# Down projections of a one-core transformer kernel: who makes the weight sums, and what tells TensorE that the token sums are there

## The reference

```
def swiglu(h, w1, w3, w2):
    return (jax.nn.silu(h @ w1) * (h @ w3)) @ w2

def conv_ffn(xn, w_up, conv_w, conv_b, w_down):
    h = causal_depthwise_conv(xn @ w_up, conv_w) + conv_b
    g, u = jnp.split(h, 2, axis=-1)
    return (jax.nn.gelu(g) * u) @ w_down
```

## Time and profile before

| | us |
|---|---|
| three executions | 2795.14, 2795.41, 2796.20 |
| the profiled execution, whole | 2793.67 |
| its span | 2791.9 |
| TensorE busy | 2723.3 (98%) |
| VectorE busy | 1519.2 (54%) |
| ScalarE busy | 471.2 (17%) |
| GpSimd busy | 109.4 (4%) |
| TensorE's share of the chain that ended last | 94% |

### The profile page before, as it was taken

How to read it: one execution, slowest core, us unless ns; L and a number is a source line. 1 busy time by engine, 2 the same in 40 slices (tenths; PEclk the granted TensorE clock), 3 DMA queues, 4 the chain that set the end, 5 groups by cost and what they waited for, 6 DMA issues and landing times.

```text
span 2791.9 us, 38954 instructions
## 1 busy us (share of the span) xinstructions
PE 2723.3 (98%) x16184; PEld 2459.8 (88%) x16184; DVE 1519.2 (54%) x3134; ACT 471.2 (17%) x827; POOL 109.4 (4%) x98
## 2 busy tenths in 40 slices
PE   7999999999999999999999999999999999999998
PEld 6899899888889999889878899988888998887888
DVE  4687765453457666466563466535335652323565
ACT  1011332321100100242132100003210011111000
POOL 0000000000000340000000131000000000000000
PEclk9999999999999999999999999999999999999999
DMA  9886621325886444441132444442324444342442
GB/s 368 316 320 253 236 91 61 114 100 178 296 303 259 161 167 167 165 149 48 61 121 106 165 168 167 156 163 104 136 106 152 159 157 151 129 146 96 154 159 95
DMA packets 74720, 460.78 MB, mean 165 GB/s; under 512 B 8340, under 2 KB 9248, under 8 KB 28208
## 3 DMA queue, kind: packets, MB, share of 16 engines
q1 hardware_dynamic: 73408, 451.44, 44.6%
q0 software_dynamic: 1136, 6.86, 0.7%
HBM read 457.17 MB, written 1.09 MB: 164 GB/s over the span
## 4 chain that ended last, share of the span: by engine, by line
PE 94%; DVE 3%; DVEq 1%; ACT 1%; DMA 1%; issue 0%; ACTq 0%
PE psum L514 20%; PE psum L560 16%; PE psum L706 14%; PE psum L646 9%; PE psum L873 8%; PE psum L947 4%; PE psum L758 4%; PE psum L595 2%; PE psum L582 2%; PE psum L661 2%; PE psum L893 2%; PE psum L823 1%; PE psum L770 1%; PE psum L536 1%; PE psum L846 1%; PE psum L836 1%
## 5 line engine op out<-in xcount | busy, mean ns | idle before, releaser
L514 PE MATMUL psum<-h,ring 128*128 128x256 f32 x1648 | 358.8, 379 | 3.1 <-DVE h L1978 1.7
L514 PEld LDWEIGHTS psum<-h,ring 128*128 128x128 f32 x1648 | 312.5, 190 | 47.8 <-DVE h L1978 2.5
L560 PE MATMUL psum<-aring,ring 128*128 128x256 f32 x1408 | 304.7, 379 | 1.7 <-issue 1.7
L560 PEld LDWEIGHTS psum<-aring,ring 128*128 128x128 f32 x1408 | 267.4, 190 | 38.7 <-issue 2.4
L706 PE MATMUL psum<-arena 128*128 128x128 f32 x2112 | 249.7, 275 | 1.1 <-DVE arena L1624 1.1
L706 PEld LDWEIGHTS psum<-arena 128*128 128x128 f32 x2112 | 242.6, 192 | 1.3 <-DVE arena L1624 1.3
L873 PE MATMUL psum<-h,ring 128*128 128x256 f32 x1024 | 231.1, 382 | 0.0
L873 PEld LDWEIGHTS psum<-h,ring 128*128 128x128 f32 x1024 | 193.2, 192 | 26.9 <-issue 1.9
L706 PE MATMUL psum<-arena,ring 128*128 128x128 f32 x1584 | 191.6, 275 | 0.0
L706 PEld LDWEIGHTS psum<-arena,ring 128*128 128x128 f32 x1584 | 184.4, 192 | 0.2
L514 PE MATMUL psum<-arena,ring 128*128 128x256 f32 x720 | 157.7, 380 | 6.0 <-DVE arena L2331 3.1
(11 more groups left out here) (417 smaller groups left out, 3567.2 us busy)
## 6 DMA issues: line engine op xcount, KB each, us to landing
ring<-wstream SPq DMA_DIRECT2D x351, 1024.0 KB, 4.8
aring<-astream SPq DMA_DIRECT2D x128, 512.0 KB, 5.3
arena<-astream SPq DMA_DIRECT2D x16, 512.0 KB, 18.0
arena<-wstream SPq DMA_DIRECT2D x3, 1024.0 KB, 20.5
arena<-decays POOLq DMA_DIRECT2D x2, 1024.0 KB, 7.7
sq<-decays POOLq DMA_DIRECT2D x2, 1024.0 KB, 5.2
kst<-const SPq DMA_DIRECT2D x1, 1280.5 KB, 7.9
x<-xT SPq DMA_DIRECT2D x1, 1024.0 KB, 4.9
```

Source lines behind the costliest of these rows:

```text
L514: mm = pe.matmul(out, lhsT=tile_at(at[0] % RING, t), rhs=rhs(k), start=k == 0, stop=k == kt - 1)
L560: mm = pe.matmul(psum[:, s % 4, n * T:(n + 1) * T], lhsT=tile_at(slot, n * KD + k), rhs=rhs(k), start=k == 0, stop=k == KD - 1)
```

## The change

All four weight sums of a down slab are made by GpSimd, in a new function `down_weight_sums`, which is put into GpSimd's queue at the place where each of the six rounds comes in the program. VectorE's `weight_sums` and its calls go. The semaphore `weights_summed` is split: `down_summed` (GpSimd, two signals a slab: third and fourth sum) and `hidden_ready` (VectorE, two signals a round: token sums up to hidden slab 15, and the last ones). TensorE waits for `down_summed` ahead of M6 and M3, for `hidden_ready` at slabs 0 and 2.

```
+            def down_weight_sums(rounds):
+
+                first = first_down[rounds]
+                for j in range(11):
+                    i = first + j
+                    w = ring[:, i % RING].rearrange("p (a t) -> p a t", a=4)
+                    new = down_sums[:, j % 2].rearrange("p a u t -> p a (u t)")
+                    pool.wait_ge(landed[i % RING], landing(i))
+                    if j >= 2:
+                        pool.wait_ge(slab_used, i - 1)
+                    nc.gpsimd.tensor_tensor(new[:, 0], w[:, 2], w[:, 3], ALU.add)
+                    nc.gpsimd.tensor_tensor(new[:, 1], w[:, 0], w[:, 2], ALU.subtract)
+                    pool.drain()
+                    nc.gpsimd.tensor_tensor(new[:, 2], new[:, 0], w[:, 0], ALU.subtract).then_inc(down_summed, 1)
+                    pool.drain()
+                    nc.gpsimd.tensor_tensor(new[:, 3], w[:, 1], new[:, 2], ALU.subtract).then_inc(down_summed, 1)
...
+            down_weight_sums(0)
             decay_rows(0)
+            down_weight_sums(1)
             for s in range(2, NF):
                 weight_sums(quick_up[0], s)
+            down_weight_sums(2)
             decay_rows(1)
             pool.wait_ge(arena_free, 1)
             pool.dma_start(memx, memT).then_inc(mem_in, 16)
             for s in range(2, NF):
                 weight_sums(quick_up[1], s)
+            down_weight_sums(3)
             for layer, n in ((0, FH), (1, LH)):
...
+                down_weight_sums(4 + layer)
...
                     if j == 0:
-                        pe.wait_ge(weights_summed, 34 * rounds + 1)
+                        pe.wait_ge(hidden_ready, 2 * rounds + 1)
...
                     if j == 2:
                         fresh()
-                        pe.wait_ge(weights_summed, 34 * rounds + 7)
+                        pe.wait_ge(hidden_ready, 2 * rounds + 2)
...
-                            need = dict(M6=2, M5=2, M7=2, M3=3).get(name, 0)
-                            if need and p == mine[0][0]:
-                                pe.wait_ge(weights_summed, 34 * rounds + 3 * j + need + (j >= 2))
+                            if name in ("M6", "M3") and p == mine[0][0]:
+                                pe.wait_ge(down_summed, 22 * rounds + 2 * j + (1 if name == "M6" else 2))
...
                 if s % 4 == 3:
                     D()
-                    token_sums(hidden, down_tokens, s // 2 - 1, 2)
-                if s in (18, 20):
-                    D()
-                    weight_sums(first, s // 2 - 9)
+                    last = token_sums(hidden, down_tokens, s // 2 - 1, 2)
+                    if s == 15:
+                        last.then_inc(hidden_ready, 1)
                 if s == NF - 1:
                     D()
-                    token_sums(hidden, down_tokens, s // 2, 1).then_inc(weights_summed, 1)
+                    token_sums(hidden, down_tokens, s // 2, 1).then_inc(hidden_ready, 1)
...
-                first = cnt.value("slab_used")
                 for j in range(11):
-                    if j + 2 < 11:
-                        weight_sums(first, j + 2)
```

More of the change, by code:

```diff
@@ L318, in build @@
         roots_read = sem("roots_read")
-        weights_summed = sem("weights_summed")
+        down_summed = sem("down_summed")
+        hidden_ready = sem("hidden_ready")
         first_sums = sem("first_sums")
@@ L1611, in token_sums, with before_down @@
                 return TT(t[:, :, 3], t[:, :, 1], v[:, :, 1, 0], ALU.subtract)
[L1613 to L1622, removed]
-                D()
[L1624 to L1628, removed]
+            def before_down(s):
                 if s % 4 == 3:
                     D()
-                    token_sums(hidden, down_tokens, s // 2 - 1, 2)
-                if s in (18, 20):
-                    D()
-                    weight_sums(first, s // 2 - 9)
+                    last = token_sums(hidden, down_tokens, s // 2 - 1, 2)
+                    if s == 15:
+                        last.then_inc(hidden_ready, 1)
                 if s == NF - 1:
                     D()
-                    token_sums(hidden, down_tokens, s // 2, 1).then_inc(weights_summed, 1)
+                    token_sums(hidden, down_tokens, s // 2, 1).then_inc(hidden_ready, 1)
             def add_products(c, low, middle, high, wait):
@@ L1691, in quick_swiglu @@
                        ALU.mult)
-                    before_down(s, first + NF)
+                    before_down(s)
                     D()
@@ L1797, in early_swiglu @@
                     ada_sums(s)
-                    before_down(s, NF)
+                    before_down(s)
                     if s == NF - 5:
@@ L1814, in swiglu @@
                     ada_sums(turn + s)
-                    before_down(s, turn + NF)
+                    before_down(s)
             def shift_column(v, n):
@@ L2268, in conv_ffn @@
                         op1=ALU.mult)
-                    before_down(s, DEPTH * SLABS_1 + (layer + 1) * (SLABS_2 // 2) - 11)
+                    before_down(s)
             def angles():
```

## The result

Medians, the ratio of the change to the kernel before, and its 95% interval.

| | us, median | ratio | 95% interval |
|---|---|---|---|
| before, 6 runs | 2795.29 | | |
| the change, 6 runs | 2805.82 | 1.0034 | 1.0023 to 1.0044 |

What follows compares the result with a forecast made beforehand. TensorE was taken to bound the kernel, busy 2723.3 us of a span of 2791.9. The terms, -1.07 + 6.2 + 0.5 = +5.6 us, took the median from 2795.41 to 2801.0 us; range 2793.8 to 2805.5.

Steps and rivals of the forecast that it cites:

- Term 1: First down round, third slab: TensorE's one stop for a VectorE weight sum goes, -1.07 us.
- Term 2: First round: GpSimd's sums delay VectorE's last token sums, so TensorE waits at the third slab; +6.2 us, ends 0 and +9.
- T_2: Start of slab j = 2, the third slab, of a down round; put at 183.5 us in the first round.
- Term 3: Rest of the first round behind that wait: GpSimd's sums late beside VectorE's products; +0.5 us, ends 0 and +1.7.
- The second round: Second down round, one condition product a slab: GpSimd keeps about 1 us in hand; cost 0, at most +1 us.
- The signs: Expected in the profile after: stretched product about 2.2 us, first sums near 155 us, 5.2 to 5.6 us a slab.
- Weight slabs up to 5 us later ... cost nothing: SyncE's weight slabs behind late condition blocks come up to 5 us later; four slabs, 25 us, of lead cover it.
- Rival B: First round: token sums stay within their 1.3 us margin, only the removed stop counts, 2794.3 us; chance 0.26.
- Rival C: Every down round: GpSimd drains cost 1 us, a slab takes 7.05 us, total 2816 us or so; chance 0.09.
- Rival D: Freed VectorE lets go of banks or vectors earlier somewhere, 7 us gained in all, 2788.4 us; chance 0.05.

Runs made afterwards that it cites:

- first_on_gpsimd: The change, but only the first down round's weight sums are on GpSimd, the other five rounds' back on VectorE; ratio 1.0031 to the kernel before.
- rest_on_gpsimd: The change, but the first down round's weight sums are back on VectorE, the other five rounds' stay on GpSimd; ratio 1.0005 to the kernel before.
- gpsimd_memsets: The change with each GpSimd addition replaced by two memsets of its output, so GpSimd reads nothing from SBUF; ratio 0.9997 to the kernel before.
- before_delayed: The kernel before, with nine extra VectorE additions ahead of the first round's last token sums, GpSimd idle there; ratio 1.0031.
- before_delayed_4: The kernel before, with five extra VectorE additions ahead of the first round's last token sums, GpSimd idle there; ratio 1.0015.
- short_products: The change with the condition products of hidden slabs 18 to 21 cut from 1024 columns to 8; ratio 1.0011 to the kernel before.
- tokens_first: The change, with VectorE making the token sums ahead of the same slab's condition products in the first network; ratio 1.003 to the kernel before.
- slab_ahead: tokens_first, with SyncE also sending each weight slab ahead of the condition blocks due before it; ratio 1.0041 to the kernel before.
- split_first: rest_on_gpsimd, with the first round split: VectorE sums slabs 0 to 2, GpSimd slabs 3 to 10; ratio 1.0027 to the kernel before.
- sums_ahead: The kernel before, with slab 2's weight sums and the token sums put ahead of the first network's last three condition products; ratio 0.9998.

## Why the prediction was right or wrong

**The check over all kernels.** For each kernel: all stops of the down projections in its trace; what the slow clock added to the pieces that ran at a granted clock below full (x12 over 1.58, x24 over 2.94, x16 over 1.95 and x10 over 1.28 us); the sum of both less the old 1.07; and the change of the time that the ratio gives.

| | stops | clock | sum | measured (interval) |
|---|---|---|---|---|
| the change | 8.1 | 2.7 | +9.7 | +9.5 (6.4 to 12.3) |
| first_on_gpsimd | 7.0 | 2.4 | +8.3 | +8.7 (5.3 to 12.3) |
| rest_on_gpsimd | 3.8 | 0 | +2.7 | +1.4 (-1.1 to 3.6) |
| gpsimd_memsets | 0.6 | 0 | -0.5 | -0.8 (-3.4 to 1.7) |
| before_delayed | 7.0 | 3.6 | +9.5 | +8.7 (5.3 to 12.0) |
| before_delayed_4 | 4.8 | 0 | +3.7 | +4.2 (1.7 to 6.7) |
| short_products | 3.6 | 0 | +2.5 | +3.1 (0.6 to 5.9) |
| tokens_first | 7.2 | 1.6 | +7.7 | +8.4 (5.3 to 11.7) |
| slab_ahead | 10.4 | 2.3 | +11.6 | +11.5 (7.8 to 15.1) |
| split_first | 5.8 | 1.7 | +6.4 | +7.5 (4.8 to 10.6) |
| sums_ahead | 1.4 | 0 | +0.3 | -0.6 (-3.1 to 1.7) |

All eleven sums lie in their intervals. The intervals reach 2.4 to 3.7 us to either side, stops and clock are those of one execution each, and the 1.07 taken off is that of one execution of before. So the table shows that no term above some 3 us is missing, and not more.

**Term 1, the stop that goes: right.** L706 <- L1624 is in no row of after. Its 1.07 us was also all that the waits of this execution offered.

**Term 2, the token sums: right in mechanism and place, and near in size, the last in part by luck.** Said 6.3 us of wait in the first round at T_2, once (the sum then took 6.2 for it); found 6.02, once. Inside: said 15 hindered operations at 1.0 us less 1.8 us of idle time used up, 13.2; found 15 that lost 12.1 (six products 0.5 to 1.07 each, two products 0.1 each, three token sums of 256 columns 0.9 to 1.1 each, the four short ones 3.9 in all), and the waits for blocks grew to 2.25 us where they were to vanish. These two errors nearly cancel. But two offsets, which the prediction didn't have, cancel in part as well. VectorE entered the stretch 1.7 us late, and TensorE was ready for the token sums at 184.37 (190.39 less 6.02) and not at 183.5. Without them the same turns would give an estimated 5 us (182.23 + 8.0 - 1.7 - 183.5); first_on_gpsimd, with the same order in that round, shows 5.38. gpsimd_memsets (0.6 us) shows that GpSimd has to read for it, short_products (no token wait) that VectorE has to be full, and before_delayed that a stop like this brings the loss with GpSimd idle.

**Term 3, the tail: the size was off.** Said 0.5, at most 1.7; the round from 201.27 on lost 2.1 us, 1.6 of it in two stops. Without the cover of the long stop it is 3.1 (short_products) to 3.5 us (split_first). The count gave 47.0 us of work for 45.3, 1.7 late at worst, and the stops of the change are just that; it was wrong to take 0.5. GpSimd never waits for a landing there: from 199.79 to 225.75 the sums of four slabs take 6.5 us each, with no wait for a slab, and TensorE takes 6.25. What makes the tail longer than the count's 1.7 us in short_products and split_first was not worked out.

**The second round: said 0, at most +1; 0.9 in the ledger**, with one stop of 0.49.

**A term was missing: TensorE's clock.** The sum took a stop of 6.3 us at its length. The matmuls behind it ran at 1.2 GHz until about 196 us and lost 2.7 us. The rows of before couldn't give this price, since their one stop was 1.07 us. But the text ahead of the prediction says that the clock of before is at full speed in all forty slices, and that reads the page wrongly: its 9 stands for 90% or more of a slice of 70 us. The windows of TensorE in the trace of before do show the lower level, though not behind a stop:

```profile
1458.00:1460.00 2.00, 2.00 (x11) 0.50 0.00 0
```

With this term and the true tail the sum is -1.07 + 6.02 + 2.7 + 2.1 + 0.9 = +10.7, the 9.8 + 0.9 of the ledger. The forecast of +5.6 was short by 3.9 us of the +9.5 measured, and 2.7 of them are this term. The upper end of the range, 2805.5, lies 0.6 us above 2804.9 and 0.3 below the median of the six runs. It was made of wider bounds for the token sums and the tail and not of the clock, so that it held the result is luck in part.

**The signs.** The product at 158.70 took 2.29 us (about 2.2 said), and GpSimd's pace is 5.33 us a slab from the third round on (5.2 to 5.6 said). GpSimd's first sum came at 157.59 (near 155 said), and it was busy for 474.7 us (some 450 said).

**"Weight slabs up to 5 us later ... cost nothing": true only behind the long stop.** In tokens_first GpSimd waited 9.2 us for three slabs from 184 us on and TensorE 5.9 for GpSimd. The lead of four slabs is that of the matmuls; the sums need a slab up to two slabs earlier, and blocks stand ahead of it in SyncE's queue.

**Rival B (not slower): refuted.** VectorE didn't win the turns, and the token sums ended 8.0 us late. **Rival C (GpSimd paces every round): refuted.** In the third round, with VectorE out of the way, the timeline of GpSimd shows the drain as 0.16 us of idle time (taken as 0.1). A slab's sums take 5.33 us, and GpSimd then waits 0.92 us for TensorE in each 6.25:

```profile
1080.35 1.26 POOL L463 TENSOR_TENSOR arena<-ring 128x512 f32<-128x512 f32 x1 [0.71 <-PE psum L728]
1084.41 1.27 POOL L468 TENSOR_TENSOR arena<-ring,arena 128x512 f32<-128x512 f32 x1 [0.16 <-issue]
1086.60 1.28 POOL L463 TENSOR_TENSOR arena<-ring 128x512 f32<-128x512 f32 x1 [0.92 <-PE psum L728]
```

**Rival D (more gained): refuted.** The kernel rest_on_gpsimd, which frees VectorE in five rounds, gains nothing.

**Left open.** A dip of the clock between 580 and 600 us (granted 0.83) and another between 1440 and 1480 start within a run of 32 one-column matmuls in a mixer. TensorE is busy then; in the change its last stop ahead of the first dip is one of 1.38 us that ends 15 us earlier. The run of 32 and the level behind it, in the timeline and the windows of the change:

```profile
585.91 4.40 PE L1081 MATMUL psum<-kst,sq 128*128 128x1 f32 x32
589.00:590.00 1.00, 1.00 (x7) 0.50 0.00 0
```

Such a dip costs some 3.3 us, the 3.3 of the ledger. The dips come and go: the profiled execution of before had only the second (0.89 from 1460 to 1480), rest_on_gpsimd and split_first neither, gpsimd_memsets both, though its one stop was 0.6 us. So they don't need the long stop of the first round. Whether it makes them likelier is open: all four kernels with a stop above 5 us show both, and of the other eight traces only that of gpsimd_memsets does. They are probably most of the spread of before's own executions: of 17 on one chip, the eight with a mean granted clock of 0.998 took 2793.2 to 2794.7 us and the nine with 0.997 or less 2795.5 to 2800.3. Nor is it settled which stops bring a dip: those of 2.04 (split_first) and 3.24 us (tokens_first) did, those of 2.23 and 2.53 (before_delayed_4) and of 2.15 (rest_on_gpsimd) didn't.

## What to carry to other kernels

Before moving work off an engine, look for the stops of the bounding engine that name this work: here they were 1.07 us of a span of 2791.9, and freeing VectorE in the other five rounds gained nothing. Two-input additions on GpSimd beside a dense VectorE cost it more than they save (12.1 us against an estimated 5.6 ahead of the token sums, about 1.07 for each pair that meets), so put them only where VectorE has room: price them at the tightest deadline, not on the average. And price a long stop of TensorE above its length: here 6.0 us of standing cost 8.7. Last, look at when the engine enters the stretch: between executions with the same order ahead of it this alone differed by 2 us.

## What the runs showed of the hardware

- GpSimd and VectorE take turns one whole operation at a time when both add SBUF operands: a 0.29 us token sum takes 1.17 to 1.34 us behind a 1.27 us GpSimd addition. With GpSimd only writing (gpsimd_memsets), the two-input products keep their 1.22 us.
- Operations with one SBUF tensor and a scalar per partition suffer too, which the prediction had not expected; beside the memsets of gpsimd_memsets their mean is 0.44 us. The groups of VectorE by line (count | busy us, mean ns | idle us before), before and then after:

```profile
L1726 DVE TENSOR_SCALAR arena<-x,mulc 128x256 f32<-128x256 f32 x24 | 7.4, 351 | 1.5
```

```profile
L1729 DVE TENSOR_SCALAR arena<-x,mulc 128x256 f32<-128x256 f32 x24 | 19.3, 842 | 1.5
```

- A drain between dependent additions of GpSimd shows as 0.16 us of idle time: the next addition starts 1.43 us after the last (1082.98 to 1084.41) where it starts 1.22 us after it without one.
- The clock can fall to half while TensorE has work: granted 0.50 from 589 to 595 us in the change and from 1458 to 1464 in before, starting within a run of 32 one-column matmuls.
